# A two-layer hybrid trunk on one core: mLSTM decay masks, packed gate weights, output gates by DMA, and value bursts changed

## The reference, cut to what matters

```python
def mlstm_chunkwise(q, k, v, i_pre, f_log, C0, n0, m0):
    ...
        b = jnp.cumsum(fb, axis=-1)
        a = b + m[..., None]
        D = jnp.where(lower, b[..., :, None] - b[..., None, :] + ib[..., None, :], -jnp.inf)
        mt = jnp.maximum(a, jnp.max(D, axis=-1))
        s = jnp.einsum('bhtd,bhsd->bhts', qb, kb) * jnp.exp(D - mt[..., None])
    ...
def merge_residual(x, ys, zs, g_merge, gate, w_branch, w_out, ln_g, ln_b, alpha):
    gates = jnp.split(jax.nn.sigmoid(g_merge), N_BRANCH, axis=-1)
    merged = sum(gb * ((yb * jax.nn.silu(zb)) @ w_branch[i])
                 for i, (yb, zb, gb) in enumerate(zip(ys, zs, gates)))
    h = alpha * x + gate * (merged @ w_out)
    return (layer_norm(h) * ln_g + ln_b).astype(x.dtype)
```

## Time and profile before

| | |
|---|---|
| median of 3 runs | 1549.59 us (1549.05 to 1552.27) |
| the profiled execution | 1550.15 us |
| its span in the trace | 1548.4 us |
| granted TensorE clock, mean | 0.999 of full speed |
| instructions in the trace | 22424 |

### The profile page before, as it was taken

One profiled execution on the slowest core, in us unless ns is written; L12 is line 12 of the kernel. 1 busy time (PEld: TensorE's weight loads), 2 busy tenths in 40 slices (PEclk: granted clock), 3 DMA queues, 4 the chain that ended last, 5 costly groups with the idle time before them and its releaser, 6 DMA issues.

```text
span 1548.4 us, 22424 instructions
## 1 busy us (share of the span) xinstructions
PE 1514.7 (98%) x8995; PEld 1248.4 (81%) x8995; DVE 731.7 (47%) x1403; ACT 464.4 (30%) x1035; POOL 643.7 (42%) x573
## 2 busy tenths in 40 slices
PE   8999999999999999999999999999999999999997
PEld 6798788886788887788878977889768888778886
DVE  5596700656423333622497584126571136262257
ACT  1246710155410123411144485012661003242010
POOL 3561045720245453155773400556204554423562
PEclk9999999999999999999999999999999999999999
DMA  9421012327222222025431100223301221211421
GB/s 338 117 72 28 1 56 81 100 68 242 81 71 71 69 68 63 27 80 179 123 126 41 52 21 15 68 82 85 111 27 56 81 82 55 69 48 50 168 82 69
DMA packets 80487, 128.71 MB, mean 83 GB/s; under 512 B 16444, under 2 KB 29184, under 8 KB 80384
## 3 DMA queue, kind: packets, MB, share of 16 engines
q1 hardware_dynamic: 78144, 122.03, 25.8%
q10 hardware_dynamic: 2240, 5.24, 0.9%
HBM read 120.96 MB, written 6.30 MB: 82 GB/s over the span
## 4 chain that ended last, share of the span: by engine, by line
PE 83%; DVE 8%; POOL 4%; issue 2%; ACT 2%; DMA 1%; POOLq 0%; DVEq 0%; ACTq 0%; SPq 0%
PE pb L1057 56%; PE pb L1202 5%; PE pb L1326 4%; PE pb L1277 3%; PE pb L1082 3%; PE pb L1245 2%; PE pb L1001 2%; PE pb L1252 1%; PE pb L1507 1%; PE pb L1370 1%; DVE ks L2173 1%; DMA raw<-in_w_mod 1%; POOL slot_T L883 1%; POOL wsp L883 1%; DVE xh L2684 0%
## 5 line engine op out<-in xcount | busy, mean ns | idle before, releaser
L1057 PE MATMUL pb<-wsp,act_T 128*128 128x512 f32 x3048 | 713.2, 391 | 3.9 <-DVE act_T L2112 1.8
L1057 PEld LDWEIGHTS pb<-wsp,act_T 128*128 128x128 f32 x3048 | 568.0, 188 | 128.3 <-issue 7.1
L880 POOL CAST wsp<-raw 128x1024 fp32r<-128x1024 f32 x128 | 136.6, 1067 | 677.4 <-PE pb L1057 588.7
L883 POOL TENSOR_TENSOR wsp<-raw,wsp 128x512 fp32r<-128x512 f32 x268 | 360.3, 1365 | 10.2
L1057 PE MATMUL pb<-wsp,yT 128*128 128x512 f32 x720 | 165.7, 389 | 0.0
L1057 PEld LDWEIGHTS pb<-wsp,yT 128*128 128x128 f32 x720 | 135.0, 188 | 27.9
L2636 DVE SCALAR_TENSOR_TENSOR mt<-tg,pb 128x512 f32<-128x512 f32 x40 | 27.4, 685 | 216.6 <-PE pb L1057 215.8
L1938 ACT ACTIVATE tg<-pb 128x512 f32<-128x512 f32 x60 | 35.9, 599 | 275.9 <-PE pb L1057 275.9
L1277 PE MATMUL pb<-ident,pr 128*128 128x128 f32 x480 | 73.4, 274 | 3.0 <-ACT pT L1819 1.9
L2335 DVE TENSOR_SCALAR pr<-pr,rden 128x640 f32<-128x640 f32 (+2 forms) x128 | 69.1, 540 | 4.5
L2636 DVE SCALAR_TENSOR_TENSOR merged<-tg,pb 128x512 f32<-128x512 f32 x20 | 13.7, 687 | 119.9 <-PE pb L1057 119.9
(11 more groups left out here) (303 smaller groups left out, 1963.7 us busy)
## 6 DMA issues: line engine op xcount, KB each, us to landing
raw<-in_w_in SPq DMA_DIRECT2D x112, 512.0 KB, 3.6
raw<-in_w_mod SPq DMA_DIRECT2D x32, 512.0 KB, 4.6
raw<-in_w_branch SPq DMA_DIRECT2D x24, 512.0 KB, 3.6
raw<-in_w_out SPq DMA_DIRECT2D x16, 512.0 KB, 3.6
stage<-in_w_mod SPq DMA_DIRECT2D x28, 256.0 KB, 7.3
raw<-in_w_in SPq DMA_DIRECT2D x16, 256.0 KB, 5.0
xh<-in_x_sample SPq DMA_DIRECT2D x6, 512.0 KB, 6.5
out<-xh ACTq DMA_DIRECT2D x5, 512.0 KB, 3.0
```

The costliest lines, as they stand in the source:

```text
L880: pool.tensor_copy(hi, raw[:, p % 3, :, 0:width]).then_inc(raw_hi, 1)
L883: ins = pool.tensor_tensor(lo[:, j, :], raw[:, p % 3, j, 0:width], hi[:, j, :].bitcast(F32), ALU.subtract)
L1057: mm = pe.matmul(dst, lhs(a, k, t), w[:, wa, j, 0:width], start=(k == 0 and n == 0), stop=(i == count - 1 and j == 1 and n == 2))
```

## The change

The output gates are no longer spread by TensorE: ScalarE waits for the two last chunks and issues 16 DMAs a layer from a row of `mrow` to 128 partitions of `gate_bc`, after its last copy of branch C. The lo parts of the gate weights lie beside the hi parts in one array (rows 4 to 7, 36 to 39, and so on), so that two matmuls a block give all; VectorE moves the lo sums onto the hi ones with a shuffle of partitions and adds both with the bias. The mask is no longer a matmul: VectorE adds it to the decay rows on the way out of PSUM, and ScalarE takes the exponential in place in SBUF. In layer 0's branch C the values of a group are computed in its part 0. Some semaphores that were one for each layer count on through both (not shown).

```diff
                                 after=next_quarter)
                     project(("A", "q"))
-                def gates():
-
-                    for i in range(4):
-                        acquire(("gate", i))
-                        which, hf = i // 2, i % 2
-                        wait_done(pe, ("gmod", len(LATE_CHUNKS[l]) - 2 + hf))
-                        for q in range(4):
-                            r = 32 * q + which
-                            mm = pe.matmul(pb[:, bank_of(("gate", i)), tile_cols(q)], ident[:, r:r + 1].to_broadcast([P, P]),
-                                           mrow[:, hf, :], start=True, stop=True)
-                        mm.then_inc(*full(("gate", i)))
-
                 def late_step(s):
                     chunks = LATE_CHUNKS[l]
...
                         if br == "A":
-                            parts = ((T, 0, 1), (), (2, 3), ())[part]
+                            parts, last = ((T, 0, 1), (), (2, 3), ())[part], (2, 3)
+                        elif l == 0:
+                            parts, last = ((T, 0, 1, 2), (), (), ())[part], (0, 2)
                         else:
-                            parts = ((T, 0), (), (1, 2), ())[part]
+                            parts, last = ((T, 0), (), (1, 2), ())[part], (2, 2)
                         for i in parts:
...
                                 mm = pe.matmul(pb[r, bank_of(key), (2 * hh + lo) * P:(2 * hh + hi) * P], v_of,
                                                pT[:, g % 2, place_of, 2 * e + lo:2 * e + hi, :]
                                                .rearrange("p u q -> p (u q)"),
-                                               start=(b == T), stop=(part == 2 and i == parts[-1]))
-                        if part == 2:
+                                               start=(b == T), stop=((part, i) == last))
+                        if part == last[0]:
                             mm.then_inc(*(full(key) if hh else (pv_group[l], 1)))
...
                         for k in range(KD):
-                            for n, (a, part) in enumerate(((0, 0), (0, 1), (1, 0))):
+                            for a in range(2):
                                 mm = pe.matmul(pb[:, bank_of(("B", "gates", i)), 0:cs.stop - cs.start],
-                                               gw[:, part, k, :], act_T[:, a, k, cs],
-                                               start=(k == 0 and n == 0), stop=(k == KD - 1 and n == 2))
+                                               gw[:, 0, k, :], act_T[:, a, k, cs],
+                                               start=(k == 0 and a == 0), stop=(k == KD - 1 and a == 1))
                         mm.then_inc(*full(("B", "gates", i)))
                     project(("B", "v"))
...
                         d = m if m < 2 else (m - 2) // MH
-                        pe.matmul(pb[:, b, :].rearrange("p (n q) -> p n q", n=LT), masks[:, 0, :],
-                                  masks[:, 3 + d, :].unsqueeze(1).to_broadcast([P, LT, P]), start=True, stop=False)
                         if m < 2:
                             for h in range(MH):
                                 c = MH * d + h
                                 mm = pe.matmul(pb[:, b, tile_cols(h)], own[0:GR2, c:c + 1].to_broadcast([GR2, P]),
-                                               RX[0:GR2, tile_cols(LT)], start=False, stop=(h == MH - 1))
+                                               RX[0:GR2, tile_cols(LT)], start=True, stop=True)
                         else:
                             c = m - 2
                             mm = pe.matmul(pb[:, b, :], own[0:GR2, c:c + 1].to_broadcast([GR2, P]),
-                                           RX[0:GR2, 0:HALF], start=False, stop=True)
+                                           RX[0:GR2, 0:HALF], start=True, stop=True)
                         mm.then_inc(*full(key))
...
-                        for i in range(4):
-                            wait_full(act, ("gate", i))
-                            act.copy(gate_bc[:, i // 2, (i % 2) * HALF:(i % 2 + 1) * HALF], bank(("gate", i)))\
-                                .then_inc(*done(("gate", i)))
+                        for hf in range(2):
+                            wait_done(act, ("gmod", len(LATE_CHUNKS[l]) - 2 + hf))
+                            for r in (32 * q + which for which in range(2) for q in range(4)):
+                                at = hf * HALF + r // 32 * P
+                                act.dma_start(gate_bc[:, r % 32, at:at + P],
+                                              mrow[r:r + 1, hf, :].unsqueeze(1).to_broadcast([1, P, P])).then_inc(gate_in, 16)
...
                     def decay(m):
-                        key = ("B", "GB", m)
-                        wait_full(act, key)
+                        wait_done(act, ("B", "GB", m))
                         if m == 0:
                             wait_done(act, ("B", "wcb"))
                         d = m if m < 2 else (m - 2) // MH
...
                             t, h = (LT, i) if m < 2 else (i, (m - 2) % MH)
                             dst = emc[:, d, h, :] if m < 2 else em[:, d, h, t, :]
                             r = ROW0[d] + h
-                            ins = act.activation(dst, pb[:, bank_of(key), tile_cols(i)], ACT.Exp,
-                                                 bias=cols[:, t, 0, r:r + 1], scale=-1.0)
-                        ins.then_inc(*done(key))
+                            ins = act.activation(dst, dst, ACT.Exp, bias=cols[:, t, 0, r:r + 1], scale=-1.0)
+                        ins.then_inc(em_ready, 1)
...
-                                wait_full(dve, ("gate", 3), l - 1)
+                                dve.wait_ge(gate_in, 16 * 16 * l)
                             take_row(("gmod", n), n)
...
                     wait_full(dve, ("C", "BR", 1, T - 1))
-                    step(dve.memset(gw[:, :, :, :].rearrange("p a k n -> p (a k n)").bitcast(F32), 0.0))
+                    step(dve.memset(gw[:, 0, :, :].rearrange("p k n -> p (k n)").bitcast(F32), 0.0))
...
                             o = 64 * g + ROW0[d]
-                            ins = dve.tensor_tensor(gw[:, 1, :, o:o + MH],
+                            ins = dve.tensor_tensor(gw[:, 0, :, o + MH:o + 2 * MH],
                                                     gwraw[:, :, (2 * d + g) * MH:(2 * d + g + 1) * MH],
                                                     gw[:, 0, :, o:o + MH].bitcast(F32), ALU.subtract)
                     ins.then_inc(gw_ready[l], 1)
-                    wait_full(dve, ("gate", 3))
                     dve.memset(v1[:, :, :, DV:DV + 1], 1.0)
                     dve.memset(RX[:, :].bitcast(F32), 0.0)
...
                     for i, cs in enumerate((slice(0, TOK // 2), slice(TOK // 2, TOK))):
                         wait_full(dve, ("B", "gates", i))
                         b, n = bank_of(("B", "gates", i)), cs.stop - cs.start
-                        dve.tensor_scalar(rw[0:GR, cs], pb[0:GR, b, 0:n], gbias[0:GR, 0:1], None, ALU.add)
-                        dve.tensor_scalar(rf[0:GR, cs], pb[64:64 + GR, b, 0:n], gbias[64:64 + GR, 0:1], None,
-                                          ALU.add).then_inc(*done(("B", "gates", i)))
+                        step(dve.stream_shuffle(r1[:, cs], pb[:, b, 0:n], [(q + MH) % 32 for q in range(32)]))
+                        dve.scalar_tensor_tensor(out=rw[0:GR, cs], in0=pb[0:GR, b, 0:n], scalar=gbias[0:GR, 0:1],
+                                                 in1=r1[0:GR, cs], op0=ALU.add, op1=ALU.add)
+                        dve.scalar_tensor_tensor(out=rf[0:GR, cs], in0=pb[64:64 + GR, b, 0:n],
+                                                 scalar=gbias[64:64 + GR, 0:1], in1=r1[64:64 + GR, cs],
+                                                 op0=ALU.add, op1=ALU.add).then_inc(*done(("B", "gates", i)))
                     wait_done(dve, ("B", "gates", 1))
...
                     dve.tensor_copy(pick[:, :, :].rearrange("p m (b q) -> p (m b) q", b=2),
-                                    own[:, :].bitcast(F32).unsqueeze(2).to_broadcast([P, 2 * MH, HD])).then_inc(pick_ready[l], 1)
+                                    own[:, :].bitcast(F32).unsqueeze(2).to_broadcast([P, 2 * MH, HD])).then_inc(pick_ready, 1)
+
+                    def decay_mask(m):
+                        key = ("B", "GB", m)
+                        d = m if m < 2 else (m - 2) // MH
+                        wait_full(dve, key)
+                        dve.tensor_tensor(emc[:, d, :, :] if m < 2 else em[:, d, (m - 2) % MH, :, :],
+                                          bank(key).rearrange("p (n q) -> p n q", n=LT),
+                                          masks[:, 3 + d, :].unsqueeze(1).to_broadcast([P, LT, P]), ALU.add)\
+                            .then_inc(*done(key))
                     def query_decay(m):
                         key = ("B", "W", m)
...
                     for n, slot in enumerate(SLOTS):
```

(25 more changed lines are left out.)

## The result

The changed kernel takes 1562.03 us (median of four runs, 1561.04 to 1563.53), the kernel before beside it 1549.32. The ratio is 1.0079, 95% interval 1.0061 to 1.0096: slower by 0.8%, about 12.7 us, where 17.6 us less had been forecast. Nearly all of the difference of 30 us has one cause. It is rival A of the prediction, and the kernel pays for it twice: 25.1 us of waiting and 4.4 us of slower clock.

The account below looks back on a forecast made before the run. The prediction took TensorE, busy 98% of the time, to bound the kernel. Savings of 7.2 + 4.7 + 4.6 + 1.4 = 17.9 us took the profiled 1550.15 to 1532.2, stated as 1532.0 for the median; range 1528 to 1538.

Parts of the forecast that it names:

- rival A: Output-gate issues, c us each, block ScalarE; TensorE stalls 16c - 11.7 us a layer, kernel slower from c = 1.3; chance 0.07.
- The gates' added cost: Output gates: 16 DMA issues a layer on ScalarE's queue, 0.44 us each, 7.0 in all, covered by the product, costing nothing.
- The 0.44 row: Profile row for a broadcast to 128 partitions, 0.44 to 0.49 us, taken as the price of one output-gate issue.
- The prediction's own sign of being wrong: At the output gates: issue rows over 0.73 us with a TensorE wait for ScalarE's tg at the branch product.
- The estimate that stood beside it: Output-gate broadcasts: by port rate, one of 64 KB reads for 2.4 us, the 16 for 19 to 38; time up to 1585.
- The gates' removed cost: Output gates: 16 matmuls a layer leave TensorE, saving 3.6 us a layer, 7.2 in both.
- the 17 named as a sign: Sign of being right: TensorE's busy time some 17 us lower over the whole kernel.
- Gate weights: Gate weights in one pass: 16 matmuls of 320 columns a layer go, 2.34 us, 4.7 in both; VectorE's added work costs nothing.
- Masks: Decay steps: ten mask matmuls a layer leave TensorE, 0.23 us each, saving 4.6 us; VectorE's ten adds cost 0.
- The slack of 0.17 us on VectorE: Decay steps: VectorE's wait before the state update of 625.11, said to absorb its being some 0.1 us behind.
- The burst: Layer 0: one value burst per group instead of two, 0.18 us saved in each of eight groups, 1.4 us.
- The sum: Whole kernel: 7.2 + 4.7 + 4.6 + 1.4 = 17.9 us saved, giving a forecast of 1532.0 us.

## Why the prediction was wrong

**The gates' added cost: the step that failed.** The prediction took 0.44 us for an issue from its nearest row and concluded "So I cost them at nothing". The issues took 1.58 and 1.51. The 0.44 row was a broadcast of a row that lies in HBM, and in the run that reads one the median issue took 0.45 (8.8 and 7.9 us for 16, for 7.0 forecast): the price was nearly right for that source and was carried over to one in a single partition of SBUF, the very thing that the text of rival A named as unseen in the trace. I set it aside because the blocked issues in the trace stood in slices of heavy DMA traffic and this place had little. But the series takes the same 25.27 us behind the TANHs as ahead of them, and with the same weight loads it goes from 33.6 to 8.8 us by the source alone. The prediction's own sign of being wrong, issue rows over 0.73 us and a TensorE wait for tg, is what the trace shows. To give 0.07 to a price that no row of such a source bounded from above, on the one engine that the branch product waits for, was the error of judgement.

**Rival A: right in mechanism and nearly in price.** Its rule, a stall of 16c - 11.7 us a layer, gives 13.6 and 12.4 at the measured c; the waits are 13.13 and 11.99, since the room is 12.1. What it lacked is the clock, 4.4 us, so that the kernel turns slower than before earlier than at its c = 1.3: with the rows alternating, at a mean of 1.18 and 1.17 us, it already stands at 1.0008 of before. With both, 1532.0 + 25.1 + 4.4 = 1561.5; measured 1562.03. The estimate that stood beside it, 19 to 38 us for the series, worked out from the port figure in the Trainium skill, "SBUF — State Buffer", section "Door 1: The DMA port swizzle", holds the 24 to 25 us measured, and its lower end is about what the alternating order came to (18.9).

**The gates' removed cost: right.** 7.2 us forecast; with the issues out of the way, 1540.09 - 1532.89 = 7.2. TensorE's busy time fell by 14.0 us, not the 17 named as a sign; without the 4.4 us that the slower clock adds to the branch product it would be 18.4.

**Gate weights: right, by the trace.** 2.34 us in layer 0, as forecast (no run puts this part back alone), and VectorE's wait of 21 us covers shuffles and adds. The shuffle took 0.53, the add that stood in for it 0.54.

**Masks: right, a little under.** 4.6 forecast, 4.7 by the trace, 5.0 by the run that puts them back. The slack of 0.17 us on VectorE is still 0.17.

**The burst: size open.** In layer 0 the way from the first scores of branch C to the start of G's last matmuls took 84.2 and 83.6 us in the two kernels with two bursts, and 82.5 to 83.4 (median 82.8) in eleven of twelve with one: 1.1 us, for 1.4 forecast. The twelfth is the run with 8 wide DMAs, 86.2, with its granted clock down to 0.91 there. But the 10.0 us of the run with the gates on TensorE, less 4.7 for the gate weights and 4.7 to 5.0 for the masks, leave it only 0.3 to 0.6. The burst was not run alone, and the spread of the single traces (0.9 us) is nearly as large as its gain.

**The sum.** The kernel that the prediction had in mind, with issues that cost nothing, is the one with the issues behind the TANHs: 1532.0 forecast, 1532.89 measured; against before beside it the gain is 17.2 us, for 17.9, with the masks a little over and the burst under their forecasts. The range of 1528 to 1538 held that kernel and not the changed one, because the bounds of the issue's cost were left to a rival that the range left out.

## What to carry to other kernels

Here the median issue of one and the same size cost its engine from 0.45 to 2.42 us, by what the broadcast read. So price an issue in a series by how fast its source can be read, and put the series where the issuing engine has idle time of its own, behind the instruction that others wait for. A price from a row of another kind of source is no bound. And where a rival's price can't be bounded by a row, the range belongs out to it, with the clock's loss added to a wait of TensorE of several microseconds.

## What was not expected of the hardware

- Broadcasts of 64 KB that all read one partition went at 27 GB/s (2.42 us each), and spread over 16 different partitions they were still slow in landing: 4.3 us against 2.2 for the same bytes read from 128 partitions.
- Exchanging rows 32 and 64 (and 33 and 65) in the order of the issues took 25.3 us down to 18.9.
- A wait of 6.4 us was enough for the granted clock to fall and the product to lose 1.5 us. Waits of 3.30 and 2.97 us in one kernel ended differently: 15.48 us in layer 0, with the granted clock at 0.50 from 438 to 440 us, and 13.88 in layer 1, with the clock at 1.00 throughout. Why is open.
- Matmuls whose result is thrown away won 4.2 us.
